# Activation tiles of an encoder step kept in three spaced blocks of columns

## The reference

```python
def swiglu_ffn(x, g, w_gate, w_up, w_down):
    h = rmsnorm(x, g)
    return (jax.nn.silu(h @ w_gate) * (h @ w_up)) @ w_down

# per layer, for xp (256 rows) and xs (32 rows, with key and value caches)
xp = xp + 0.5 * swiglu_ffn(xp, *ffn1)
op, sp = mixer_prompt(rmsnorm(xp, norm_gains[l, 1]), *lw)   # z = h @ w_in; three attention groups;
xp = xp + op                                                # concat(A, B, C) @ w_out
xp = xp + 0.5 * swiglu_ffn(xp, *ffn2)
```

## Time and profile before

| | |
|---|---|
| median of 3 runs | 2054.03 us |
| profiled execution | 2054.93 us |
| its span | 2053.4 us |
| PE busy | 2046.0 us (100%) |
| PEld busy | 2026.2 us (99%) |
| DVE busy | 1170.1 us (57%) |
| ACT busy | 846.2 us (41%) |
| granted TensorE clock | 1.000 |
| DMA, mean | 166 GB/s |

### The profile page before, as it was taken

One profiled execution on the slowest core, in us unless ns is written; L12 is line 12 of the kernel. 1 busy time (PEld: TensorE's weight loads), 2 busy tenths in 40 slices (PEclk: granted clock), 3 DMA queues, 4 the chain that ended last, 5 costly groups with the idle time before them and its releaser, 6 DMA issues.

```text
span 2053.4 us, 41905 instructions
## 1 busy us (share of the span) xinstructions
PE 2046.0 (100%) x15805; PEld 2026.2 (99%) x15805; DVE 1170.1 (57%) x1790; ACT 846.2 (41%) x1290; POOL 88.5 (4%) x140
## 2 busy tenths in 40 slices
PE   9999999999999999999999999999999999999999
PEld 8999999999999999999999999999999999999999
DVE  7555445554455556588889755555445555455544
ACT  6333333333333344345668644333333333333332
POOL 0000000000000000022432000000000000000000
PEclk9999999999999999999999999999999999999999
DMA  7544555545545545544443455555544555545554
GB/s 260 164 163 160 173 163 170 171 162 161 176 158 170 169 156 178 178 143 157 152 153 111 148 164 164 167 170 168 172 160 164 168 166 168 171 163 165 168 183 144
DMA packets 101274, 339.96 MB, mean 166 GB/s; under 512 B 12149, under 2 KB 16293, under 8 KB 101200
## 3 DMA queue, kind: packets, MB, share of 16 engines
q1 hardware_dynamic: 95856, 329.41, 49.0%
q0 software_dynamic: 2960, 7.45, 1.3%
q10 hardware_dynamic: 2400, 2.33, 0.3%
HBM read 334.45 MB, written 5.28 MB: 165 GB/s over the span
## 4 chain that ended last, share of the span: by engine, by line
PE 97%; DVE 1%; ACT 1%; issue 0%; DMA 0%; SPq 0%; DVEq 0%; ACTq 0%
PE bank L601 31%; PE bank L603 31%; PE bank L602 31%; PE bank L688 1%; PE bank L721 1%; PE bank L703 1%; PE bank L665 0%; DMA raw<-in_w_ffn_up 0%; DVE w_lo L1367 0%; PE bank L903 0%; ACT w_hi L1056 0%; ACT s_buf L1113 0%; PE bank L705 0%; DVE z_prep L1448 0%; ACT z_prep L1113 0%
## 5 line engine op out<-in xcount | busy, mean ns | idle before, releaser
L601 PE MATMUL bank<-h_hi,w_hi 128*128 128x288 f32 x3344 | 989.4, 296 | 2.3 <-DVE w_lo L1624 2.0
L603 PE MATMUL bank<-h_lo,w_hi 128*128 128x288 f32 x3344 | 986.3, 295 | 0.0
L602 PE MATMUL bank<-h_hi,w_lo 128*128 128x288 f32 x3344 | 985.1, 295 | 0.0
L1367 DVE TENSOR_TENSOR w_lo<-raw,w_hi 128x1024 fp32r<-128x1024 f32 x634 | 729.7, 1191 | 206.6 <-ACT w_hi L1056 206.2
L1056 ACT ACTIVATE w_hi<-raw 128x1024 fp32r<-128x1024 f32 x634 | 617.0, 1020 | 321.0 <-PE bank L603 318.2
L601 PEld LDWEIGHTS bank<-h_hi,w_hi 128*128 128x128 f32 x3344 | 628.7, 188 | 6.9 <-DVE w_lo L1624 3.2
L602 PEld LDWEIGHTS bank<-h_hi,w_lo 128*128 128x128 f32 x3344 | 628.9, 188 | 0.2
L603 PEld LDWEIGHTS bank<-h_lo,w_hi 128*128 128x128 f32 x3344 | 628.8, 188 | 0.0
L603 PE MATMUL bank<-gu_lo,w_hi 128*128 128x288 f32 x1376 | 405.9, 295 | 0.0
L601 PE MATMUL bank<-gu_hi,w_hi 128*128 128x288 f32 x1376 | 405.2, 294 | 0.0
L602 PE MATMUL bank<-gu_hi,w_lo 128*128 128x288 f32 x1376 | 405.2, 294 | 0.0
(11 more groups left out here) (205 smaller groups left out, 985.6 us busy)
## 6 DMA issues: line engine op xcount, KB each, us to landing
raw<-in_w_ffn_gate SPq DMA_DIRECT2D x168, 512.0 KB, 4.5
raw<-in_w_ffn_up SPq DMA_DIRECT2D x168, 512.0 KB, 4.6
raw<-in_w_ffn_down SPq DMA_DIRECT2D x96, 512.0 KB, 3.8
raw<-in_w_in SPq DMA_DIRECT2D x74, 512.0 KB, 4.7
raw<-in_w_ffn_down SPq DMA_DIRECT2D x64, 384.0 KB, 4.2
raw<-in_w_out SPq DMA_DIRECT2D x32, 512.0 KB, 4.5
raw<-in_w_ffn_down SPq DMA_DIRECT2D x32, 448.0 KB, 4.4
bias_rev<-bias_vectors POOLq DMA_DIRECT2D x11, 256.0 KB, 4.6
```

What stands on the lines that cost most here:

```text
L601: pe.matmul(out, w_hi[b][:, k, :], hi, start=(k == first_k), stop=False)
L602: pe.matmul(out, w_lo[b][:, k, :], hi, start=False, stop=False)
L603: mm = pe.matmul(out, w_hi[b][:, k, :], lo, start=False, stop=(k == last_k))
L1367: dve.tensor_tensor(w_lo[b][:, k, :], raw_tile(ph, j, s)[:, k, :], w_hi[b][:, k, :].bitcast(F32), ALU.subtract)\
```

## The change

The room of 320 numbers for a tile stays, and so do all addresses of tensors. In it the 288 columns are kept as three blocks of 96 columns. The first begins 4 numbers (16 bytes) into the room, and each next one begins 104 numbers after the one before, which leaves 8 unused numbers (32 bytes) between blocks. `right_side` now gives a view of four axes (partition, tile, block, column). Every instruction that writes such a tile uses that view for its output, with its inputs cut into the same blocks by `blocks`. TensorE reads the blocks in the forward direction, and the output row in PSUM is written forward too: there the three blocks touch, so the built instruction has the plain pattern [1, 288] for its output, and [104, 3] [1, 96] for its right side, where it had [-1, 288] for both. The scratch `key_hi` and `key_lo` is now the first 288 numbers of tile 5's room.

No instruction is added, removed or moved: on every engine the same instructions stand in the same order, and on SP, POOL and PE their rows are the same in every word.

```diff
         def right_side(name, tiles, scope=ctx):
             room = sb(name, [P, tiles, TILE], F32R, scope)
-            return room[:, :, PAD:PAD + NT], room
-
-        TILE = -(-NT // 64) * 64
-        PAD = 24
+            spread = room[:, :, PAD:PAD + NT // BLOCK * APART].rearrange("p t (a b) -> p t a b", b=APART)
+            return spread[:, :, :, 0:BLOCK], room
+
+        def blocks(row):
+            return row.rearrange("p (a b) -> p a b", b=BLOCK)
+
+        BLOCK, APART, TILE, PAD = 96, 104, 320, 4
...
-        key_hi, key_lo = o_hi[:, 5, :], o_lo[:, 5, :]
+        key_hi, key_lo = o_hi_room[:, 5, 0:NT], o_lo_room[:, 5, 0:NT]
...
-                    hi, lo = (t[:, ::-1] for t in rhs(k))
+                    hi, lo = rhs(k)
                     b = buf(ph, s)
-                    out = (bank or bank_w[b])[:, 0:NT][:, ::-1]
+                    out = blocks((bank or bank_w[b])[:, 0:NT])
                     pe.matmul(out, w_hi[b][:, k, :], hi, start=(k == first_k), stop=False)
                     pe.matmul(out, w_lo[b][:, k, :], hi, start=False, stop=False)
                     mm = pe.matmul(out, w_hi[b][:, k, :], lo, start=False, stop=(k == last_k))
...
             def h_rhs(k):
-                return h_hi[:, k, :], h_lo[:, k, :]
+                return h_hi[:, k, :, :], h_lo[:, k, :, :]
...
-                        act.activation(gu_hi[:, j, :], gu[:, :], ACT.Copy).then_inc(guh_rdy, 1)
+                        act.activation(gu_hi[:, j, :, :], blocks(gu[:, :]), ACT.Copy).then_inc(guh_rdy, 1)
...
-                        dve.tensor_tensor(gu_lo[:, j, :], gu[:, :], gu_hi[:, j, :].bitcast(F32), ALU.subtract).then_inc(gul_rdy, 1)
+                        dve.tensor_tensor(gu_lo[:, j, :, :], blocks(gu[:, :]), gu_hi[:, j, :, :].bitcast(F32), ALU.subtract).then_inc(gul_rdy, 1)
```

More of the change, by code:

```diff
@@ L160, in encoder_step @@
             gu_lo, _ = right_side("gu_lo", thirds[0], ffn_scope)
-        o_hi, _ = right_side("o_hi", 16)
-        o_lo, _ = right_side("o_lo", 16)
+        o_hi, o_hi_room = right_side("o_hi", 16)
+        o_lo, o_lo_room = right_side("o_lo", 16)
         ident = sb("ident", [P, P])
@@ L1065, in h_upper @@
             def h_upper(index, j):
-                act.activation(h_hi[:, j, :], xT[:, j, :], ACT.Copy, scale=g_cols[:, bass.ds(j + index * DT, 1)]).then_inc(hhi_rdy, 1)
+                act.activation(h_hi[:, j, :, :], blocks(xT[:, j, :]), ACT.Copy, scale=g_cols[:, bass.ds(j + index * DT, 1)]).then_inc(hhi_rdy, 1)
             def x_norm(index):
@@ L1135, in out_hi @@
                 act.wait_ge(pv_done, U + (3 * p + 3))
-                act.activation(o_hi[:, tile, :], bank_o[:, 0:NT], ACT.Copy).then_inc(ohi_rdy, 1)
+                act.activation(o_hi[:, tile, :, :], blocks(bank_o[:, 0:NT]), ACT.Copy).then_inc(ohi_rdy, 1)
             def prep_items(step):
@@ L1375, in h_tile @@
                 dve.wait_ge(hhi_rdy, H + 1)
-                dve.scalar_tensor_tensor(h_lo[:, j, :], xT[:, j, :], g_cols[:, bass.ds(j + index * DT, 1)],
-                                         h_hi[:, j, :].bitcast(F32), ALU.mult, ALU.subtract).then_inc(hlo_rdy, 1)
+                dve.scalar_tensor_tensor(h_lo[:, j, :, :], blocks(xT[:, j, :]), g_cols[:, bass.ds(j + index * DT, 1)],
+                                         h_hi[:, j, :, :].bitcast(F32), ALU.mult, ALU.subtract).then_inc(hlo_rdy, 1)
             def x_norm(index, n):
@@ L1488, in out_lo @@
                 dve.wait_ge(ohi_rdy, body * 2 + (p + 1))
-                dve.tensor_tensor(o_lo[:, tile, :], bank_o[:, 0:NT], o_hi[:, tile, :].bitcast(F32), ALU.subtract).then_inc(olo_rdy, 1)
+                dve.tensor_tensor(o_lo[:, tile, :, :], blocks(bank_o[:, 0:NT]), o_hi[:, tile, :, :].bitcast(F32), ALU.subtract).then_inc(olo_rdy, 1)
             def attention_pairs(body, splits, reads, tiles, sums, late):
@@ L1615, in lower @@
                     dve.wait_ge(hhi_rdy, t + 1)
-                    dve.scalar_tensor_tensor(h_lo[:, t, :], xT[:, t, :], g_cols[:, t:t + 1], h_hi[:, t, :].bitcast(F32),
+                    dve.scalar_tensor_tensor(h_lo[:, t, :, :], blocks(xT[:, t, :]), g_cols[:, t:t + 1], h_hi[:, t, :, :].bitcast(F32),
                                              ALU.mult, ALU.subtract).then_inc(hlo_rdy, 1)
```

4 lines of the change are left out of this document (2 added, 2 removed).

## The result

The changed kernel takes 2114.72 us, the median of 4 runs (2102.11 to 2114.92), against 2053.97 us for the kernel before. The ratio is 1.028, with an interval of 1.0242 to 1.0318. It is slower by 60.7 us, where 2035 us and a range up to 2080 were forecast. Three of the four runs lie within 0.3 us of each other; the fourth, 2102.11 us, is 12.6 us faster and was not traced. The profiled execution took 2114.81 us, its span is 2113.2 us, and the granted clock is 1.000.

The account below looks back on a forecast made before the run. TensorE's matmul pitch was taken to bound the kernel. From the 2053.4 us span, 19 us for the jumps came off, other terms being 0; with 1.5 us around it, 2035.9, median 2035 us, range 1988 to 2080.

Parts of the forecast that it names:

- What bounds the kernel: TensorE never runs out of work; 14928 main matmuls at a pitch of 131.12 ns take 1957 us, 95% of the span.
- The part that depends on the layout: Of each main matmul's pitch, at most 11.1 ns surplus could depend on where columns lie; 10 ns was used.
- Item 1: Main matmuls read and written forward instead of reversed: no change, taken as 0.
- Item 2: Jumps between blocks of the right side skip part of an assumed read drift, gaining 1.25 ns a matmul, 19 us.
- Item 3: ScalarE and VectorE writing tiles in three blocks: taken as 0, at worst 21 us showing.
- Item 4: Weight supply for strips of 48 matmuls: nothing becomes late, so no gain is given back by another engine.
- Rival A: The layout changes nothing, the surplus per matmul being a fixed cost: 2054 us, chance 0.15.
- Rival B: Each jump in the right side stalls the stream one step, 25 us, 2079 us; two steps 2104; chance 0.28 with D.
- D: Writers of tiles come late, up to 21 us, 2075 us if the pitch stays; chance 0.02, counted with B.
- Rival C: Collisions of right-side and weight reads nearly vanish at the jumps: 5 ns a matmul, 75 us, 1979 us; chance 0.13.

Follow-up runs that it names:

- the series: Kernel before with series of 96 matmuls in many layouts appended behind its last strip; only pitches read: 131.1 ns layout before, 135.6 changed blocks.
- the sixth experiment: Kernel before, read and written forward, contiguous from column 4 in place of 24: 2061.95 us, ratio 1.0027.
- the last experiment: Changed kernel with one more fp32r matmul of 48 columns behind each L651, into unused columns: 2102.38 us, ratio 1.02.

## Why the prediction was wrong, by its own steps

*What bounds the kernel.* Right. TensorE's pitch sets the time: every result here follows from counts in windows, and the working by pitch gives 59.9 us where the span grew by 59.8.

*The part that depends on the layout.* "At most 11.1 ns, I work with 10" was a bound and holds for the gain: the best layout found takes 1.1 ns out. The error is the picture behind it, of a hindrance that one can take out by eighths. A stream of these matmuls settles on a repeating pattern; the pitches found most often at 288 columns are 130.0, 131.1, 131.7, 133.3, 135.6 and 140.0 ns. In steps of 0.83 ns they are 156, 157.3, 158, 160, 162.7 and 168, with thirds where three matmuls together take a whole number of steps.

*Item 1, direction alone, 0.* Wrong: 10 or 20 us more from 24, by the run. L663 and L664, which answer to the earlier trace rows with the columns still together, take 0.13 and 0.13 us in the trace of after:

```profile
955.32 0.30 PE L663 MATMUL bank<-o_hi,mean_hd 128*128 128x288 f32 x1
955.45 0.29 PE L664 MATMUL bank<-o_lo,mean_hd 128*128 128x288 f32 x1
955.58 0.39 PE L668 MATMUL bank<-mean_hd,z_prep 128*128 128x2 f32 x3
```

The rows could not tell 0.55 ns from nothing, and two matmuls between others do not show what a long stream settles on. The 130 to 140 ns read from them did hold the result, but the nearest value was taken for the likely one.

*Item 2, the jumps, -19 us.* This is the step that failed. It put a gain of 1.25 ns a matmul on the jumps; in the changed kernel, forward and from 4, they cost 53 us, 3.5 ns a matmul. It had two parts, and both fell. That weights and right side drift past each other at 1.2 against 2.4 columns a nanosecond, with a wait in proportion to it, would bring the surplus down to a quarter with 32 weight columns in place of 128. At 288 columns the pitch of the layout before rose by 2.2 ns and that of the blocks fell by as much; at 256 columns it fell from 119.95 to 113.5 ns, which halves the surplus over the 106.7 ns of 256 columns at 2.4 a nanosecond. The weight load does matter, but not in that proportion. That a jump takes out a piece of the wait would show in either direction; reversed, the jumps moved the time by 0.45 us, forward from 4 they cost 53 us, and from 0 and 8 there are runs at 130.0 ns. The prediction also has no item for the start, which the change moves from 24 to 4: it stood at nothing without a reason. Undone one at a time, by the medians, the change is: start 24 to 4, +32 us reversed; the gaps, 0 behind it; forward instead of reversed, +28 us. In the other order: forward +15, start to 4 -7, gaps +53. The parts do not add up to prices of their own, so a sum by parts could have met the total only by luck.

*Item 3, the writers, 0.* Right, to 1 ns in three rows.

*Item 4, weight supply.* Right: the wait of L604 is 0.8 us in all, and at the faster pitch of 130.0 ns nothing became late either.

*Rival A, no change.* Wrong here. The Trainium skill, "SBUF — State Buffer", section "Who interferes with whom", calls the two read ports of TensorE independent. Weights shifted in their tile by 24 numbers (L1036 of the series) changed the layout before from 131.1 to 133.3 ns, with the right side where it was. This does not show a shared port, but the timing of the two is not independent.

*Rival B, a jump costs time.* Right in sign, and its 2104 is the nearest of the numbers given, yet its mechanism, a price for each jump, is refuted by the same runs: five jumps a matmul are 16 us faster than none. That its 2104 came near is luck. B and D together were given 0.28, and the range ended at its cheaper half, 2080, because a price of one step a jump looked more natural than two. Nothing in the rows supported that choice.

*Rival C.* Its remark that such a cause would be lumpy and not even was the right one. It was used only for a gain, though lumps have no sign.

*What stays open.* What in the chip makes the pattern, and why steps of 0.83 ns. That the pitch can change where the stream is interrupted is shown by the series, by L651 in two traces and by the pause of 0.41 us; what in an interruption selects the new pitch is not. The same kind of entry did not always lead to the same pitch in a kernel (130.0, then 131.7 behind L651 in the sixth experiment). A stream without weight loads was not tried. The levels at 2039 and 2079 us of the blocks from 0 and 8, 2053 and 2074 of the forward kernels, 2088 and 2129 of the last experiment, and the changed kernel's own 2102 were not traced.

## What to carry to other kernels

Where a dense stream of matmuls sets the time, read its pitch (the distance from one start to the next) from counts in long windows and compare it in several stretches: two values in one trace, or runs at levels that are apart by a fixed amount, suggest that the stream can settle on more than one pattern. In this kernel the pitch depended on where the right side starts, its gaps and its direction at once, so an argument about one of them is worth little; measure candidate layouts in bare series, each behind several entries, and take one that has a single, fast pitch behind all. A single series promises too much, as 130.0 ns for a layout that then ran at 131.7 in the kernel.

## What the runs showed of the hardware that was not expected

- The pitch by width, contiguous from 0, with 128 weight columns: 119.95 ns at 256 columns, 120.0 at 264, 125.3 at 272, 127.8 at 280, 131.7 at 288, 136.0 at 296, 146.66 at 320. Under 256 it does not fall below 111.3 ns (128, 192 and 224 columns). The series of 320, 256 and 128 columns:

```profile
2634.80 14.24 PE L1048 MATMUL bank<-h_hi,w_hi 128*128 128x320 f32 x96
2648.88 11.68 PE L1049 MATMUL bank<-h_hi,w_hi 128*128 128x256 f32 x96
...
2681.81 10.85 PE L1052 MATMUL bank<-h_hi,w_hi 128*128 128x128 f32 x96
```

- That floor belongs to the weight load: with 32 weight columns 128 columns take 60.0 ns and 256 take 113.5, in the other set of series:

```profile
2491.74 5.92 PE L1036 MATMUL bank<-h_hi,w_hi 128*32 128x128 f32 x96
...
2505.98 11.06 PE L1038 MATMUL bank<-h_hi,w_hi 128*32 128x256 f32 x96
```

- The Trainium skill, "TensorE: Matmul & The Clock Gate", section "Back-to-back issue gap", gives N / 2.4 + 2.5 ns, and says itself that it is for an isolated matmul, a condition that the prediction left out when it set the formula against the stream's 131.1 ns. By it 256 columns would take 109.2 ns and 320 take 135.8; measured in a stream with weight loads are 119.95 and 146.66, 10.8 ns more in both.
